# Layer B attention with V as the weights of 256-query value products, 64-row scores, and projections woven between its steps

## What is computed

```python
q, k, v, g = jnp.split(u @ w_in, 4, axis=-1)           # uc @ w_in gives kc, vc
s = einsum('bnqhd,brnjhd->bhnqrj', q_r, k_reg) * scale  # 8 rows of the 64-wide grid around the query
s = s + bias[row, column];  s = where(col_mask, s, NEG_INF)
s_ctx = einsum('bnqhd,bchd->bhnqc', q_r, kc) * scale
p = softmax(concatenate([s, s_ctx]))
o = p_lat @ v_reg + p_ctx @ vc
y = (o * silu(g)) @ w_out
```

## Time and profile before

| | |
|---|---|
| median of 3 runs | 3609.2 us (3608.79 to 3617.47) |
| span of the profiled execution | 3614.6 us |
| PE, DVE, ACT busy in it | 3300.8, 1918.7, 1224.6 us |
| layer B: first tile of its projections to its last value product | 2601.5 to 3453.4 us |

### The profile page before, as it was taken

One profiled execution on the slowest core, in us unless ns is written; L12 is line 12 of the kernel. 1 busy time (PEld: TensorE's weight loads), 2 busy tenths in 40 slices (PEclk: granted clock), 3 DMA queues, 4 the chain that ended last, 5 costly groups with the idle time before them and its releaser, 6 DMA issues.

```text
span 3614.6 us, 53582 instructions
## 1 busy us (share of the span) xinstructions
PE 3300.8 (91%) x19064; PEld 2868.2 (79%) x19064; DVE 1918.7 (53%) x3829; ACT 1224.6 (34%) x2043; POOL 881.6 (24%) x324
## 2 busy tenths in 40 slices
PE   8999999888888888999799989999799999999997
PEld 6878888777777777877588878887688888888875
DVE  4676566566666666014655545544564444444444
ACT  3343344333333333012344434430243333344302
POOL 2454344422222222334211010013111111111120
PEclk9899999999999999999799999999699999999997
DMA  2011011222222224411200010042021111010321
GB/s 99 35 46 46 35 41 41 102 86 75 76 81 81 81 79 176 156 65 47 93 33 33 27 39 28 27 172 78 14 79 45 45 39 39 29 39 33 115 93 58
DMA packets 63267, 235.80 MB, mean 65 GB/s; under 512 B 7216, under 2 KB 8240, under 8 KB 62144
## 3 DMA queue, kind: packets, MB, share of 16 engines
q10 hardware_dynamic: 32352, 118.58, 8.7%
q1 hardware_dynamic: 30816, 115.91, 8.7%
HBM read 184.06 MB, written 50.40 MB: 65 GB/s over the span
## 4 chain that ended last, share of the span: by engine, by line
PE 62%; DVE 17%; issue 11%; DVEq 5%; ACT 4%; DMA 1%; ACTq 1%; SPq 0%
PE ps L163 33%; PE ps L725 10%; PE ps L702 6%; DVE fox_l L978 4%; PE ps L120 3%; PE ps L686 2%; PE ps L359 2%; PE ps L687 2%; DVEq L524 2%; DVE fx_k2b L992 1%; DVE lev L503 1%; DVE nf_tri L1002 1%; PE ps L709 1%; DVE lev L514 1%; PE ps L372 1%
## 5 line engine op out<-in xcount | busy, mean ns | idle before, releaser
L184 POOL TENSOR_TENSOR w_hi<-raw,small 128x1024 fp32r<-128x1024 f32 x160 | 459.8, 2874 | 2632.1 <-PE ps L163 2526.0
L186 POOL TENSOR_TENSOR w_lo<-raw,w_hi 128x1024 fp32r<-128x1024 f32 x160 | 422.1, 2638 | 22.8
L163 PE MATMUL ps<-u_hi,w_hi 128*128 128x512 f32 x1040 | 415.0, 399 | 12.4 <-DVE u_lo L243 7.8
L163 PE MATMUL ps<-u_lo,w_hi 128*128 128x512 f32 x1040 | 410.5, 395 | 0.0
L163 PE MATMUL ps<-u_hi,w_lo 128*128 128x512 f32 x1040 | 410.5, 395 | 0.0
L163 PE MATMUL ps<-nb_u_hi,w_hi 128*128 128x512 f32 (+1 forms) x640 | 241.0, 377 | 10.2 <-DVE nb_u_lo L1389 9.9
L163 PEld LDWEIGHTS ps<-u_hi,w_hi 128*128 128x128 f32 x1040 | 197.4, 190 | 61.7 <-issue 10.6
L163 PE MATMUL ps<-nb_u_hi,w_lo 128*128 128x512 f32 (+1 forms) x640 | 237.9, 372 | 0.0
L163 PE MATMUL ps<-nb_u_lo,w_hi 128*128 128x512 f32 (+1 forms) x640 | 237.6, 371 | 0.0
L163 PEld LDWEIGHTS ps<-u_hi,w_lo 128*128 128x128 f32 x1040 | 197.5, 190 | 44.3
L163 PEld LDWEIGHTS ps<-u_lo,w_hi 128*128 128x128 f32 x1040 | 197.7, 190 | 41.9
(11 more groups left out here) (326 smaller groups left out, 7355.5 us busy)
## 6 DMA issues: line engine op xcount, KB each, us to landing
raw<-in_w_stream SPq DMA_DIRECT2D x160, 512.0 KB, 3.5
ada_w<-in_w_ada ACTq DMA_DIRECT2D x48, 512.0 KB, 6.1
nf_b<-nf_rows ACTq DMA_DIRECT2D x16, 512.0 KB, 5.7
nb_bias<-in_rel_bias ACTq DMA_DIRECT2D x16, 448.0 KB, 3.5
y_parts<-wa_y_hi ACTq DMA_DIRECT2D x8, 640.0 KB, 3.0
y_parts<-wa_y_lo ACTq DMA_DIRECT2D x8, 640.0 KB, 4.1
la_out_yh<-y_parts SPq DMA_DIRECT2D x8, 640.0 KB, 10.0
la_out_yl<-y_parts SPq DMA_DIRECT2D x8, 640.0 KB, 11.2
```

The lines of the kernel that those rows point to most:

```text
L163: mm = pe.matmul(out, w(slot, tiles[i]), u[:, first + i, cols], start=start and i == 0 and p == 0, stop=stop and i == len(tiles) - 1 and p ...
L184: pool.tensor_tensor(w_hi[:, s, :], raw[:, s, :], zero, ALU.add)
L186: pool.tensor_tensor(w_lo[:, s, :], raw[:, s, :], w_hi[:, s, :].bitcast(F32), ALU.subtract).then_inc(w_ready, 1)
```

## The change

`nb` becomes a `Flow`, which writes out every step of all 8 turns, without a loop. Layer A and everything else stay as they are.

- **Segments and groups.** The 8 blocks are taken in four segments of two: (0, 1), (2, 3), (6, 7), (4, 5). A group is 4 transposes of one block of 128 keys for two heads and two query blocks (or of two blocks of keys that only one query block sees). There are 6, 7, 6 and 7 groups.
- **Value products.** V, split in hi and lo side by side, is the 128 weight columns; the transposed probabilities, split in hi (ACT) and lo (DVE), are the moving operand: 2 matmuls of 256 queries for each head (L1138). The output lies with head columns on partitions, its hi and lo parts on different halves, and is added up by a copy of ACT and an addition of DVE (step O). The reciprocal of the row's sum is turned by PE (L1125) and multiplied in. No output is transposed.
- **Scores.** Each head's Q and K lie on its own 64 partitions. A score step (L1104) is one piece (512 columns, then the rest) of a block for both heads: three products hi x hi, lo x hi, hi x lo on 64 rows, the heads in turn, into one bank each. A score step waits until the step before has been read (`nb_shifted`). The middle blocks are now 640 + 256 = 896 wide.
- **Weaving.** Turn t holds the projections V and G of its own pair and Q and K of the next pair. 72 matmuls (V) lie between the four score steps of the first segment; 90 are dealt out over the 26 groups, 3 or 4 after each; 72 follow the last product. Q and K of pair 0 stand in front of the first turn. There are two projection banks instead of eight columns of banks; a chunk waits until the one two before it has been taken out (`nb_act_out`, `nb_dve_out`).
- **Bias.** DMA of the next pair's bias and its additions stand at the end of a turn (step B), between two evacuations of K.

```diff
+        class Flow:
...
+            def seg_groups(self, seg):
+
+                where = {}
+                for qi, blk in enumerate(self.segments[seg]):
+                    for l0, vb in blk["chunks"]:
+                        where.setdefault(vb, {})[qi] = l0
+                both = [vb for vb in where if len(where[vb]) == 2]
+                alone = [vb for vb in where if len(where[vb]) == 1]
+                groups = []
+                for vb in both:
+                    items = [(hd, qi, where[vb][qi]) for hd in range(2) for qi in range(2)]
+                    groups.append((items, [(0, CH, vb, 0, 0)] if self.shared else
+                                   [(2 * P * hd, 2 * P, vb, hd, 2 * P * hd) for hd in range(2)]))
+                for i in range(0, len(alone), 2):
+                    items, adds = [], []
+                    for vb in alone[i:i + 2]:
+                        (qi, l0), = where[vb].items()
+                        for hd in range(2):
+                            adds.append((P * len(items), P, vb, hd, 2 * P * hd + P * qi))
+                            items.append((hd, qi, l0))
+                    groups.append((items, adds))
+                return groups
...
+                        score(s)
+                    fill_to(lead)
+                    values = [ch for ch in fill if ch["kind"] == "V"]
+                    for ch in values:
+                        if ch is values[-1]:
+                            fill_to(at["fill"] + 6)
+                        steps.append(("T", group("VT", it, chunk=ch)))
...
+                        for i, (items, adds) in enumerate(rows):
+                            g = group("P", it, seg=seg, seg_n=count["seg"], items=items, adds=adds, starts=i == 0,
+                                      ends=i == len(rows) - 1, exped=base_u + self.first_unit(seg + 1))
+                            steps.append(("T", g))
+                            l_turned[seg % 2] = g["n"] + 1
+                            share = -(-len(pending) // (len(rows) - i))
+                            for s in pending[:share]:
+                                score(s)
+                            del pending[:share]
+                            if waiting:
+                                steps.append(("V", waiting))
+                                if waiting["ends"]:
+                                    owed.append((waiting["seg"], waiting["seg_n"]))
+                            waiting = g
+                            done += 1
+                            fill_to(start + (main - start) * done // n_groups)
+                            if i == min(1, len(rows) - 1):
+                                steps.append(("I", seg, g["exped"]))
+                                norms.append((seg, g["seg_n"]))
+                            elif norms and i >= min(3, len(rows) - 1):
+                                s0, s_n = norms.pop(0)
+                                steps.append(("T", group("N", it, seg=s0, seg_n=s_n)))
+                            elif owed and owed[0] not in norms and i:
+                                steps.append(("O", it, *owed.pop(0)))
+                    steps.append(("V", waiting))
+                    owed.append((waiting["seg"], waiting["seg_n"]))
+                    fill_to(at["fill"] + 6)
+                    for s0, s_n in norms:
+                        steps.append(("T", group("N", it, seg=s0, seg_n=s_n)))
+                    fill_to(at["fill"] + 12)
+                    for s0, s_n in owed:
+                        steps.append(("O", it, s0, s_n))
+                    steps.append(("Y", it))
+                    fill_to(at["fill"] + FULL)
+                    steps.append(("D", it))
+                    if it + 1 < len(turns):
+                        steps.append(("B", it + 1, count["S"]))
+                    fill_to(FULL * len(fill))
...
+                    elif step[0] == "S":
+                        s = step[1]
+                        pe.wait_ge(self.shifted, s["n"] - 1)
+                        if s["head"]:
+                            pe.wait_ge(*s["ready"])
+                            for sm, w in before(s):
+                                pe.wait_ge(sm, w)
+                        runs = s["blk"]["pieces"][s["piece"]]["runs"]
+                        kv = self.kv_of(s["it"])
+                        qc = slice(s["blk"]["b"] * P, (s["blk"]["b"] + 1) * P)
+                        for o0, key, n in runs:
+                            for p, (q, k) in enumerate(((self.q_hi, self.k_hi[kv]), (self.q_lo, self.k_hi[kv]),
+                                                        (self.q_hi, self.k_lo[kv]))):
+                                for hd in range(2):
+                                    r = rows_of(hd)
+                                    o = (self.s_bank + hd) * CH + o0
+                                    mm = pe.matmul(ps[:, o:o + n], q[r, qc], k[r, key:key + n],
+                                                   start=p == 0, stop=p == 2)
+                        mm.then_inc(self.scored, 1)
...
+                    elif step[0] == "V":
+                        g = step[1]
+                        pe.wait_ge(self.freed, g["n"] + 1)
+                        if g["starts"]:
+                            pe.wait_ge(self.left, max(g["seg_n"] - 2, 0))
+                        o = (self.o_bank + g["seg_n"] % 2) * CH
+                        kv = self.kv_of(g["it"])
+                        for j, (p0, n, vb, hd, o0) in enumerate(g["adds"]):
+                            for part, pt in enumerate((self.pt_hi, self.pt_lo)):
+                                mm = pe.matmul(ps[:, o + o0:o + o0 + n], self.v[:, vb, kv if self.shared else hd, :],
+                                               pt[:, g["high"] % 2, p0:p0 + n],
+                                               start=g["starts"] and j == 0 and part == 0,
+                                               stop=g["ends"] and j == len(g["adds"]) - 1 and part == 1)
+                        if g["ends"]:
+                            mm.then_inc(self.summed, 1)
...
+            def act(self, act, steps, evacuate, load):
+                for step in steps:
+                    if step[0] == "S" and step[1]["end"]:
+                        s = step[1]
+                        act.wait_ge(self.shifted, s["n"])
+                        w = s["blk"]["width"]
+                        for hd in range(2):
+                            l = self.l_of(s["seg"], s["qi"], hd)[:, 0:w]
+                            nc.scalar.activation(l, l, ACT.Exp, scale=-1.0, bias=self.nm[:, s["u"] + hd, 0:1],
+                                                 accum_out=self.rs[:, s["u"] + hd:s["u"] + hd + 1]
+                                                 ).then_inc(self.exped, 1)
+                    elif step[0] == "T" and step[1]["kind"] != "N":
+                        g = step[1]
+                        act.wait_ge(self.turned, g["n"] + 1)
+                        t = (self.t_bank + g["n"] % 2) * CH
+                        if g["kind"] == "P":
+                            w = P * len(g["items"])
+                            nc.scalar.copy(self.pt_hi[:, g["high"] % 2, 0:w], ps[:, t:t + w]).then_inc(self.high, 1)
+                        else:
+                            b0, n = g["chunk"]["c0"] // P, g["chunk"]["n"]
+                            nc.scalar.copy(self.v[:, b0:b0 + n // P, :, 0:HD],
+                                           ps[:, t:t + n].rearrange("p (j h d) -> p j h d", h=2, d=HD)
+                                           ).then_inc(self.high, 1)
...
         def near_block(b):

             rs = min(max(2 * b - 4, 0), 8)
-            n = (9 if 2 <= b <= 5 else 8) * GRID_W
-            chunks = [(c * P, P, 8 + c) for c in range(2)]
-            chunks += [(C + c * P, min(P, n - c * P), rs // 2 + c) for c in range((n + P - 1) // P)]
-            return {"b": b, "width": C + n, "first": 0, "chunks": chunks, "first_row": rs - 2 * b,
-                    "runs": [(0, T, C), (C, rs * GRID_W, CH - C), (CH, rs * GRID_W + CH - C, n + C - CH)]}
+            n = 5 if 2 <= b <= 5 else 4
+            tail = [(0, rs * GRID_W + CH, P), (P, T, C)] if n == 5 else [(0, T, C)]
+            return {"b": b, "width": n * P + C, "mid": n == 5, "first_row": rs - 2 * b,
+                    "chunks": [(c * P, rs // 2 + c) for c in range(n)] + [(n * P + c * P, 8 + c) for c in range(2)],
+                    "pieces": [{"l0": 0, "runs": [(0, rs * GRID_W, CH)]}, {"l0": CH, "runs": tail}]}

...
+        nb = Flow("nb", [[near_block(b), near_block(b + 1)] for b in (0, 2, 6, 4)], False)
+        nb.allocate_first(ph7, T, TC)
+        nb.allocate(ph7, TC, [(0, CH + C), (4 * (CH + C), NEAR_W + C)] * 2, 4 * (CH + C) + 4 * (NEAR_W + C))
...
+        nb.plan(nb_units(0, "QK"),
+                [nb_units(it, "VG") + (nb_units(it + 1, "QK") if it + 1 < PAIRS else []) for it in range(PAIRS)],
```

(1 more changed line is left out.)

449 lines of the change are left out of this document (362 added, 87 removed).

## The result

The changed kernel takes 3738.4 us (median, 3731.1 to 3746.7) against 3612.0 for the kernel before in the same series: ratio 1.035, 95% interval 1.033 to 1.038. The forecast was 3665, range 3588 to 3715: the direction was right, the size was not, and the range did not hold it.

A forecast was written before the change was run, and what follows sets the result against it. PE bounded the kernel before; after, ordered waits would outweigh the PE work saved. Start, seven turns of 108.9 us and a last of 86.3 sum to 869.9 against 816.5; with 2.3 at the end, +56 on 3609.2: 3665, range 3588 to 3715.

The forecast's parts named there:

- The exponentials' chain: Attention: two exponentials (2.1 us) stand ahead of the next copy on ACT, then subtraction, shift-and-max and score step follow in order.
- the turn's end: Between turns: bias landing and additions on DVE delay K's evacuation to 18 us, so PE waits 4 us before V.
- the ends of the layer: Layer B's start: K's matmuls come later, 14.7 us, 2 for clock, 4.6 for a late bias; last turn 86.3 us.
- the clock: Rival, 0.10: after waits of 4 us or more PE runs some 20 matmuls at half clock, 4 us a turn: 3695.
- The bound of 6: Upper end of PE's forecast wait between turns, 2 to 6 us, as the bias addition ranges from 0.76 to 2.45.
- 2.3 more from last product to low part: Behind layer B's last value product: 6.6 us to the low part, where the kernel before took 4.3.
- the loop: Attention, two groups: ordered waits on ACT, DVE and score steps sum to 7.8 us, in which PE has 6.3.
- the main case: Whole kernel, chance 0.58: work falls a little, ordered waits take more; a turn of 108.9 us, 3665 in all.
- The overlap of row halves: Scores on 64 rows: partial overlap, 0.32 us a 512-column pair, between 0.229 side by side and 0.457 one after another.
- its own test: Sign against the forecast: score pairs of 512 columns every 0.23 us would make the overlap term wrong.
- the mixed case: Halves side by side, same order of waits: loop 6.9, a turn 102.3 us, 3614 in all; no chance of its own.
- the lead: Turn's start: 72 projections 13.9, four score steps 4.2, V's transposes and six projections 2.5, a wait 0.4: 21.0 us.

The follow-up runs named there:

- e4_exps_later: Changed kernel with ACT taking a block's two exponentials one at a time, each behind the next group's copy of the probabilities' high part: 3713.1 us.
- e5_together: Changed kernel with earlier bias DMAs, the last turn's G at the other turns' pace, and both exponentials behind the next group's copy from the second segment on: 3585.2 us.
- e1_bias_dma: Changed kernel with only the two DMAs of the next turn's bias table moved earlier, right behind the turn's last score step: 3657.8 us.
- e7_filled_wait: Changed kernel with 36 products of 512 columns that nothing reads put on PE in its wait at each turn's end: 3723.5 us.
- e3_loads_early: Changed kernel with the last turn's projections spread at the other turns' rate, so G and the loads waiting for it come earlier: 3715.7 us.

## Why the prediction was wrong

Its span, step by step: 27.6 for seven turns, 25.8 for start and last turn, 2.3 behind it, 55.7 in all. Measured: 78.8, 27.0, 19.3, and 5.2 of spread.

- **Right: what the bound is.** PE's work falls by a few us a turn, the ordered waits take more. Value products are 0.119 apart (0.118 forecast) and 0.112 for 128 queries; DVE is busy 60.4 us a turn (62). The exponentials' chain is the one described: e4_exps_later and e5_together show it. PE idles 17.6 us in turn 1, where 8 to 12 were forecast; 4.7 of it is the longer wait at the turn's end.
- **Right: the ends of the layer**, 27.0 for 25.8, and by the parts named: PE waits 11.3 us for Q's evacuation beside the normalisation, and K's 72 products then take 16.4 us (13.9 and 2 for the clock).
- **Wrong in size: "the turn's end", 4.0.** It is 8.7 (8.7 x 7 = 61 of e1_bias_dma's 81 us). The mechanism was named, its prices were too low. From the last product, the low part is ready after 7.4 us (6.6), the bias has landed at 14.4 (11.4: issue and flight are 6.0, where 3.5 was read from other landings), K's low part is done at 22.4 (18). The additions came to 7.2 for 5.7, but by the wrong ones: 5.6 for the first two (2.1) and 1.6 for the others (3.6). The two errors are one: GpSimd's split starts at 14.0, so additions begun at 11.4 would have been through at 13.5 (an estimate, with 1.06 each), and begun at 14.4 they meet it. The long values in the earlier trace rows were this collision too: the additions of 2.45 us start while GpSimd splits weights. The range was taken as a mean, without asking what made it. The bound of 6 let only the additions vary, not the landing. 4.7 x 7 = 33 us.
- **Wrong in choice: the clock.** It was a rival of 0.10, worth 4 us a turn at a wait of 4 or more. At 8.7 it came, and cost 2.0 to 2.5 a turn, some 15 us in all (e7_filled_wait). The Trainium skill, TensorE: Matmul & The Clock Gate, Part 1, has a clock lost in an idle stretch return with sustained work; the 0.51 and then 1.00 of the windows above agree. Its chance hung on the step before: the turn before the change, with its shorter waits, is at 1.00.
- **Wrong step: "2.3 more from last product to low part".** The end costs 19.3. That the projections of the last turn, now woven to its end, hold `w_used` back and with it SyncE's 14 loads, was not in the forecast at all, though the queue's wait stands in the code: 17 us, and e3_loads_early takes 16.3 of them away.
- **Wrong, and hidden by luck: the loop.** Without pause and clock a turn is 105.1 us (e1_bias_dma), just the 108.9 - 4.0 = 104.9 of the main case, but its terms were off both ways. The overlap of row halves, taken as 0.32 for a pair of 512 columns, is 0.34 for the first pair and 0.23 after it; by its own test that term is wrong. The second score step of a middle block takes 0.97 us, not 1.7, and the loop of two groups 7.05, not 7.8 (6.9 in the mixed case), so segment 1 of turn 1 takes 17.4 for 18.8. The mixed case, which had this overlap, is nevertheless further off: 102.3, or 98.3 without its pause. It took 2.1 us off the lead and so left nothing for changing to 64 rows and back, which costs about 0.4 us a step here and not 0.24: the four score steps cost the lead 3.7 us, and it stays at 20.9 (21.0). In segments 2 and 3, 19.8 and 19.1 (17.8 and 17.3 in the mixed case, 18.7 and 19.1 in the main one), an output step stands inside the loop: 0.8 us of copies on ACT and 1.4 us on DVE between two shift-and-max. The two exponentials take 2.1 us, as forecast: the reading of the sum, 0.19 in the trace, lies beside the next instruction.

Turns 7.3 x 7 = 51 and the end 17 make up nearly all of the 75 us between 56 and 130.

## What to carry to other kernels

When a loop is rewritten into one long program order, list for each queue what is now behind every wait for a DMA: here two loads a turn issued some 27 us sooner gave 81 us in all, and the loads behind a "last weights used" gave 23. A saving on the bounding engine shows only after the waits are taken out: the same change is 3.5% slower as written and 0.7% faster with three edits of order that take no work away. And a duration with two values in a profile is a question: ask which engine was beside it before pricing a moved instruction by its mean. The chain of waits doesn't name that engine: the end of the pause stood still while the landing moved by 1.3 us.
